# Layout of the even input projection's last 712 columns, and order of the second up chunk's matmuls

## What is computed

```
# first block, per layer (D_FF = 2816)
h = rms_norm(x, norm_ffn[l])
up = h @ w_up[l]; a, b = up[..., :D_FF], up[..., D_FF:]
x = x + (silu(conv3(a) + conv_b) * b) @ w_down[l]
# second block, layer 0 ("even")
z = rms_norm_2(x, g[0]) @ w_in                  # 1024 x 2760
q_a, c_kv, q_i, k_i, w_i, q_b, k_b, v_b = split(z, [512, 128, 512, 64, 8, 512, 512, 512])
score = sum_h relu(q_i . k_i) * w_i;  sel = top_k(score, 64)      # per query
o_a = attention over the selected tokens;  o_b = differential attention (q_b, k_b, v_b)
y = concat(o_a, o_b) @ w_out
```

## Time and profile before

| | |
|---|---|
| median of three runs | 1357.84 us |
| the profiled execution | 1359.49 us |
| its span from first to last instruction | 1357.7 us |
| granted TensorE clock, mean | 0.999 |
| busy: TensorE, VectorE, ScalarE, GpSimd | 99%, 72%, 54%, 9% |
| matmuls | 7451 |
| HBM read | 239 MB |

### The profile page before, as it was taken

One profiled execution on the slowest core, in us unless ns is written; L12 is line 12 of the kernel. 1 busy time (PEld: TensorE's weight loads), 2 busy tenths in 40 slices (PEclk: granted clock), 3 DMA queues, 4 the chain that ended last, 5 costly groups with the idle time before them and its releaser, 6 DMA issues.

```text
span 1357.7 us, 19403 instructions
## 1 busy us (share of the span) xinstructions
PE 1343.6 (99%) x7451; PEld 1130.6 (83%) x7451; DVE 979.1 (72%) x1510; ACT 738.3 (54%) x1153; POOL 125.0 (9%) x113
## 2 busy tenths in 40 slices
PE   9999999999999999999999999999999999999998
PEld 6788888888888888888888877888888878888886
DVE  5657878777665767877778687886667887776665
ACT  4565545455454754545555675654445675654443
POOL 0000002111000000211110102220000001400000
PEclk9999999999999999999999999999999999999999
DMA  8844356555555434766655623458875525366552
GB/s 280 273 155 155 126 185 215 188 187 186 186 188 184 156 124 156 227 199 198 198 186 186 185 94 126 140 202 216 219 215 189 169 95 163 118 192 203 193 190 89
DMA packets 146577, 242.25 MB, mean 178 GB/s; under 512 B 4603, under 2 KB 91403, under 8 KB 146222
## 3 DMA queue, kind: packets, MB, share of 16 engines
q1 hardware_dynamic: 142498, 226.97, 51.3%
q0 software_dynamic: 3712, 13.77, 3.8%
q10 hardware_dynamic: 276, 0.27, 0.1%
HBM read 239.03 MB, written 1.97 MB: 178 GB/s over the span
## 4 chain that ended last, share of the span: by engine, by line
PE 95%; DVE 2%; ACT 1%; DMA 1%; issue 1%; POOL 0%; DVEq 0%; ACTq 0%; POOLq 0%; SPq 0%
PE ps L1205 19%; PE ps L1143 16%; PE ps L1149 16%; PE ps L1152 16%; PE ps L1212 10%; PE ps L1311 3%; PE ps L1437 2%; PE ps L1406 1%; PE ps L1388 1%; PE ps L2050 1%; DMA raw<-in_w_in 1%; PE ps L1250 1%; PE ps L1247 1%; PE ps L1253 1%; PE ps L1589 1%; PE ps L2060 1%
## 5 line engine op out<-in xcount | busy, mean ns | idle before, releaser
L2740 DVE TENSOR_TENSOR wlo<-raw,whi 128x1024 fp32r<-128x1024 f32 (+2 forms) x423 | 510.5, 1218 | 270.7 <-ACT whi L2172 269.9
L2172 ACT CAST whi<-raw 128x1024 fp32r<-128x1024 f32 (+1 forms) x431 | 444.3, 1041 | 339.4 <-PE ps L1212 188.6
L1205 PE MATMUL ps<-act,whi 128*128 128x512 f32 x1120 | 266.4, 390 | 0.0
L1205 PEld LDWEIGHTS ps<-act,whi 128*128 128x128 f32 x1120 | 208.4, 188 | 42.2
L1143 PE MATMUL ps<-whi,mhi 128*128 128x512 f32 (+2 forms) x688 | 235.9, 392 | 0.0
L1149 PE MATMUL ps<-wlo,mhi 128*128 128x512 f32 (+2 forms) x688 | 231.1, 385 | 0.0
L1152 PE MATMUL ps<-whi,mlo 128*128 128x512 f32 (+2 forms) x688 | 231.0, 385 | 0.0
L1152 PEld LDWEIGHTS ps<-whi,mlo 128*128 128x128 f32 x688 | 129.3, 188 | 26.4
L1149 PEld LDWEIGHTS ps<-wlo,mhi 128*128 128x128 f32 x688 | 129.3, 188 | 25.9 <-DVE wlo L2740 0.4
L1212 PEld LDWEIGHTS ps<-act,wlo 128*128 128x128 f32 x1120 | 143.6, 191 | 5.5
L1143 PEld LDWEIGHTS ps<-whi,mhi 128*128 128x128 f32 x688 | 125.7, 189 | 23.7 <-issue 2.6
(11 more groups left out here) (338 smaller groups left out, 1538.9 us busy)
## 6 DMA issues: line engine op xcount, KB each, us to landing
raw<-in_mlp_w SPq DMA_DIRECT2D x64, 1024.0 KB, 5.2
raw<-in_w_up SPq DMA_DIRECT2D x44, 1024.0 KB, 5.2
raw<-in_w_in SPq DMA_DIRECT2D x38, 1024.0 KB, 5.1
raw<-in_w_down SPq DMA_DIRECT2D x22, 1024.0 KB, 5.0
raw<-in_ev_w_in SPq DMA_DIRECT2D x10, 1024.0 KB, 5.1
raw<-in_w_out SPq DMA_DIRECT2D x8, 1024.0 KB, 5.1
raw<-in_xa_wkv SPq DMA_DIRECT2D x4, 1024.0 KB, 5.5
raw<-in_ev_w_out SPq DMA_DIRECT2D x4, 1024.0 KB, 5.2
```

The source lines that it names most:

```text
L1205: nc.tensor.matmul(ps[:, bank0 + f, :], of(whi, h)[:, k, f * P:f * P + P], act2[:, kx].rearrange("p i n -> p (i n)"), start=kx == 0, stop= ...
L2172: nc.scalar.copy(whi[:, m % HL, 0:w], raw[:, n % RAW, h * w:h * w + w]).then_inc(hi_done, 1)
L2740: nc.vector.tensor_tensor(wlo[:, m % HL, 0:w], raw[:, n % RAW, h * w:h * w + w], whi[:, m % HL, 0:w].bitcast(F32), ALU.subtract).then_inc( ...
```

## The change

The even projection's columns 2048 to 2760 become two jobs of 356 columns (2048 and 2404) instead of 512 and 200. The odd projection's jobs stay as they are. `turned_chunk` gets an argument `low_first`, which is set for the second chunk of each up block: it then does the 16 matmuls of 256 columns (low weights) before the 16 of 512 (high weights). The `pe_out` increments come behind the part that is last, four per chunk as before. `turned_chunk` without it issues what it did.

```diff
+IN2_SPANS = [(512 * j, 512) for j in range(4)] + [(2048, 356), (2404, 356)], [(0, 512), (512, 512), (1024, 256)]
...
-            plan.job(("in2", l, j), wide(w, 512 * j, min(512, cols - 512 * j)))
+            plan.job(("in2", l, j), wide(w, *IN2_SPANS[l % 2][j]))
...
-                for h in range(2):
+                def high_weights(h, first, last):
                     pe.wait_ge(hi_done, 2 * n + h + 1)
                     for f in range(2):
                         for k in range(kh):
                             kx = kh * h + k
-                            nc.tensor.matmul(ps[:, bank0 + f, :], of(whi, h)[:, k, f * P:f * P + P],
-                                             act2[:, kx].rearrange("p i n -> p (i n)"), start=kx == 0, stop=False)
-                for h in range(2):
+                            mm = nc.tensor.matmul(ps[:, bank0 + f, :], of(whi, h)[:, k, f * P:f * P + P],
+                                                  act2[:, kx].rearrange("p i n -> p (i n)"), start=first and kx == 0, stop=last and kx == KD - 1,
+                                                  skip_group_check=last)
+                        if last:
+                            mm.then_inc(pe_out, 1)
+
+                def low_weights(h, first, last):
                     wait_lo(pe, 2 * n + h)
...
+                for i, part in enumerate((low_weights, high_weights) if low_first else (high_weights, low_weights)):
+                    for h in range(2):
+                        part(h, i == 0, i == 1)
...
-                    turned_chunk(nb, 4)
+                    turned_chunk(nb, 4, low_first=True)
...
-                    n = min(512, cols - 512 * j)
+                    _, n = IN2_SPANS[l % 2][j]
...
-                    n = min(512, cols - 512 * j)
-                    scaled(("in2", l, j), ("x2", l), lambda tt: proj[:, tt, 512 * j:512 * j + n], n, in2_banks(l, order.index(j)))
+                    c0, n = IN2_SPANS[l % 2][j]
+                    scaled(("in2", l, j), ("x2", l), lambda tt: proj[:, tt, c0:c0 + n], n, in2_banks(l, order.index(j)))
```

More of the change, by code:

```diff
@@ L207, in build_network @@
             plan.group(("x2", l, g), "split")
-        w, cols = (a["ev_w_in_2"][0], EV_COLS) if even else (a["od_w_in_2"][0], OD_COLS)
+        w = a["ev_w_in_2"][0] if even else a["od_w_in_2"][0]
         for j in IN2_ORDER[l % 2]:
-            plan.job(("in2", l, j), wide(w, 512 * j, min(512, cols - 512 * j)))
+            plan.job(("in2", l, j), wide(w, *IN2_SPANS[l % 2][j]))
         for keys in (EVEN_GROUPS if even else ODD_GROUPS).values():
@@ L1188, in turned_half, with turned_chunk @@
                             mm.then_inc(pe_out, 1)
-            def turned_chunk(n, bank0, stream=None):
+            def turned_chunk(n, bank0, stream=None, low_first=False):
                 if stream:
@@ L1212, in turned_chunk @@
                             mm = nc.tensor.matmul(ps[:, bank0 + f, 0:SEQ], of(wlo, h)[:, k, f * P:f * P + P], act2[:, kx, 0],
-                                                  start=False, stop=kx == KD - 1)
-                        mm.then_inc(pe_out, 1)
+                                                  start=first and kx == 0, stop=kx == KD - 1)
+                        if last:
+                            mm.then_inc(pe_out, 1)
+                for i, part in enumerate((low_weights, high_weights) if low_first else (high_weights, low_weights)):
+                    for h in range(2):
+                        part(h, i == 0, i == 1)
             def spread_row(key, l):
@@ L1748, in _ @@
                 memory_half(l, "v", 1, 6, sm)
-                cols = EV_COLS if even else OD_COLS
                 order = IN2_ORDER[l % 2]
```

## The result

The changed kernel takes **1360.44 us** in the median of 22 runs (1359.05 to 1362.01), the kernel before 1357.48 (1356.69 to 1358.16, 22 runs beside them): ratio 1.0020, 95% interval 1.0015 to 1.0026, 2.96 us more. The forecast was 1359.0 within 1356.9 to 1360.5. The sum behind it was +1.2 us, so the direction was right, the result lies 0.06 us inside the upper end of the range, and the sum missed 1.8 us.

The account below looks back on a forecast made before the run. TensorE, 99% busy, was taken to bound the kernel. Projection +1.44, up-chunk order -0.66 and stalls +0.4 gave +1.2 us, added to the 1357.84 median: 1359.0 us, range 1356.9 to 1360.5.

Parts of the forecast that it names:

- The sum: Whole kernel: +1.44 for the projection, -0.66 and +0.4 for the up chunks, +1.2 us in all.
- What bounds it: Whole span: TensorE, 99% busy with 95% of the chain, sets the time; any wait put on it lengthens the run.
- Part 1, matmul price: Even projection: 356-column matmuls cost 0.162 us each; a job 4 half drops 0.79 us, a job 5 half grows 0.60.
- the rival of dearer 356s: Three halves after the second scores: 356-column matmuls cost more than the line says, total +3.6, 1361.4 us; chance 0.05.
- the 0.75 us: Even projection: saving on TensorE alone from replacing 512 and 200 columns by 356 and 356.
- The aside: Even projection: the skill's gap rule gives 0.151 us per 356-column matmul, saving 1.05 us more; not used in the sum.
- Part 1, the wait: Even projection: TensorE waits over 2 us for VectorE before or inside the second scores; fifth scores come 1.44 us later.
- the rival in which it is swallowed: Attention behind the projection: its own waits absorb the delay, projection change about +0.3, total 0, 1357.8 us; chance 0.11.
- the rival on part 2: Up chunks: the 0.03 us belongs to the chunk's start and stays, total +1.9, 1359.7 us; chance 0.05.
- Part 2: Up chunks: one 256-to-512 switch fewer saves 0.03 us in each of 22 blocks, -0.66; two stalls add 0.4 us.
- The stalls: Third block of each layer: VectorE's low part comes late, about 0.2 us each, +0.4 in all.
- The fourth rival: Up chunks: the 0.03 us is not of the width change and stays, total +1.9, 1359.7 us; chance 0.05.

Follow-up runs that it names:

- e1: Changed kernel with the old up-chunk order restored, keeping the 356 and 356 columns: 1358.90 us, ratio 1.0015 to the kernel before.
- e2: Changed kernel with 512 and 200 columns restored, keeping the new order of the second up chunk: 1357.73 us, ratio 1.0003 to the kernel before.
- e3: e1 plus nine 512-column matmuls, result unread, on TensorE ahead of the second scores: 1359.17 us.
- e11: Whole changed kernel plus nine matmuls into an unused bank ahead of the second scores: 1359.51 us.
- e5: e1 with VectorE's last two low parts of job 5 moved behind the first and second score reductions: 1358.10 us, ratio 1.0005 to the kernel before.
- the table of widths: Old up-chunk order with other widths, against the kernel before: 456/256 ratio 0.9997, 400/312 1.0010, 300/412 1.0037; also lists e1 and e2.

## Why the forecast was right and where it was not

**What bounds it**: right. What TensorE loses up to the fifth scores in e1, 1.66 us, is what its stage loses, and from the first matmul of the out projection to the end of the span it is 530.3 us before, after and in e1.

**Part 1, matmul price**: right. The halves took 2.03 and 2.04 us where 2.83 - 0.79 = 2.04 and 1.43 + 0.60 = 2.03 were worked out; the rival of dearer 356s is out. What the 0.75 us rest on is worth a look: columns and matmuls are as many before and after, so a price that rises evenly with the columns saves nothing. The rows save because the 200s, at 0.112 us, lie 0.015 above the line through 256 and 512. The aside that the saving would be 1.05 us larger puts 0.151 us for the 356s beside the rows' prices for the 512s and 200s, and so compares two price lists.

**Part 1, the wait**: right in place, cause and size. TensorE waits 1.98 + 0.20 us (forecast: over 2), ended by VectorE; the low parts take 0.90; the first reduction begins 1.02 us after the mask (forecast 1.1); the first scores come 3.39 us earlier (3.3). Without the fall the fifth scores are later by 27.87 - 26.21 = 1.66 us, where the sum had 1.44. The term that was short by most is the second pair of scores: I gave it half of 0.85, 0.43, and it takes 798.09 to 798.72, 0.63. It is the half whose matmuls have 256 columns (the row of 798.09), not 128, and it starts behind a wait. That is +0.20 us. The way from there to the fifth scores, 798.72 to 807.45, is 8.73 us where it was 6.82 (801.83 to 808.65), 1.91 more and not 1.80: +0.11. And the pair itself came 0.08 us sooner than worked out. Together they make the 0.22. The delay then passes whole to the end, so the rival in which it is swallowed is out.

**The missing step**: I counted what the wait costs as time and not what it does to TensorE. All my durations came from rows at a granted clock of 1.00, and nothing in this stage of before has TensorE idle for 2 us, so the price of an idle stretch was never bounded. The trace of before does hold one such stretch elsewhere, the 1.99 us ahead of 37.77, and behind it the clock was 1.00 and the matmuls 0.23 us apart; it would have shown no price. So 2 us of idle time don't always bring the fall; whether the place decides or the single execution is open. In the profiled execution of the changed kernel the price is 0.15 us on the second pair of scores (0.85 instead of 0.70) and 3.52 - 2.14 = 1.38 on the half behind, 1.5 in all: 3.16 - 1.66. Over the executions the groups are 1361.03 - 1359.38 = 1.65 us apart and the upper holds 12 of 22, which puts the median in it. That the median still lies in the range is in part luck. The range's upper end was set by the rival on part 2, the upper group's own median lies above it, and +2.96 us is more than the 2.7 us that I had taken for the least that can be told from nothing; I had given that 0.06, and only for dearer matmuls.

**Part 2**: the sum had -0.66 + 0.4 = -0.26; by its measured parts it is -0.44 + 0.68 = +0.24, and by the stages of e2 +0.23. The block is shorter by 0.02 us, not 0.03: 22 x 0.02 = 0.44. I had said that 0.03 was the difference of two rounded windows and still took all of it. The stalls are 0.34 each, 0.68, in the two places named. I took the time from the low part's end to the need of the matmul, and the hand-over cost more than the remainder allowed for. The fourth rival, that the saving isn't there, is out.

**Sum with measured sizes**: +1.66 + 0.24 = +1.9 us without the fall, +3.4 with it. The groups of the changed kernel lie at +1.9 and +3.55 over the 1357.48 of before. The forecast's +1.2 was 0.7 short of the first and knew nothing of the second.

**The rival theory** of the experiments falls by e2 (no execution with a low clock in part 2), by e3 and e11, and by e5 and the table of widths, where low clocks are frequent only with the long waits. Against the loads and the other engines as the cause stand the six executions of e1 without the fall and e3, which keeps both as they were. What stays open is why the same wait of 2 us is followed by the fall in one execution and not in the next, and what made the two high times of e11.

The Trainium skill (TensorE: Matmul & The Clock Gate, Part 1: The HAM clock gate) says that the moment at which the gate acts is not tied to the kernel's own time and differs from run to run. The two groups fit that; no run here tests it.

## What to carry to other kernels

Where a kernel keeps TensorE 99% busy, a saving ahead of an engine that is level with it turns into a wait, and work that was moved behind that wait is paid in full: compare not the sums of columns but what lies ahead of and behind the next hand-over. Such a wait may cost more than its length: here an idle stretch of 2 us was followed in half of the executions by a low clock, which in the profiled one meant 3.5 us almost wholly at 1.2 GHz, 1.5 us more. When single times of a kernel form two groups, look up the granted clock of each before explaining the median, and keep an engine's shrunken job just wide enough (456 here, not 356) that the follower has arrived.

## What the runs showed of the hardware

- Granted clock and idle time of TensorE ahead of the second scores, amid work that fills 99% of the span: with none, 0 or 1 of 11 executions show a mean clock under 0.999, with 0.37 us 0 of 11, with 0.89 us 2 of 11, with 1.98 us 18 of 33, with 3.15 us 5 of 5. Idle time elsewhere did not count alike: every kernel's trace has two waits of about 0.9 us later in the stage (at 821.24 and 824.65 before, clock 1.00 behind both), and the kernel before has the one of 1.99 us at 37.77 with the clock at 1.00 behind it. In the two profiled executions that show it, the clock is 0.57 for the 3.5 and 4.0 us of the half behind the wait, and 1.00 right after. With matmuls of no use in the wait it was 1 of 22.
- The clock began to fall when TensorE was already at work again: the first pair of scores, right behind the idle time, ran at 1.00, the second pair at 0.77. With 300 columns and 3.15 us of idle time the second pair, 0.63 us, ran at 1.00 too, and only the half behind it was slow.
- The switch from 256 to 512 columns costs 0.02 us as a block of 16.57 us shows it (16.55 with one such switch fewer), not the 0.03 that two windows had suggested.
